# Two-layer trunk on one core: five of sixteen low weight parts in gate and up made by ScalarE's negated copy and an accumulating DMA inside SBUF

## The reference

```
x = x + concatenate([tok, cross]) @ w_out
x = x + swiglu(rms_norm(x, norm_ffn_g[i]), ffn_w_gate[i], ffn_w_up[i], ffn_w_down[i])
swiglu(h, w_gate, w_up, w_down) = (silu(h @ w_gate) * (h @ w_up)) @ w_down
```

## Time and profile before

| | |
|---|---|
| median of 3 runs | 2358.95 us |
| lowest and highest | 2358.91, 2359.38 us |
| profiled execution, span of its instructions | 2357.9 us |
| VectorE busy | 1734.6 us (74%) |
| ScalarE busy | 1239.5 us (53%) |
| GpSimd busy | 159.7 us (7%) |
| DMA | 441.14 MB, mean 187 GB/s |

### The profile page before, as it was taken

How to read it: one execution, slowest core, us unless ns; L and a number is a source line. 1 busy time by engine, 2 the same in 40 slices (tenths; PEclk the granted TensorE clock), 3 DMA queues, 4 the chain that set the end, 5 groups by cost and what they waited for, 6 DMA issues and landing times.

```text
span 2357.9 us, 29177 instructions
## 1 busy us (share of the span) xinstructions
PE 2350.1 (100%) x10566; PEld 1902.8 (81%) x10566; DVE 1734.6 (74%) x2131; ACT 1239.5 (53%) x1545; POOL 159.7 (7%) x114
## 2 busy tenths in 40 slices
PE   9999999999999999999999999999999999999999
PEld 7888888888788888888888888888888888888887
DVE  6555666656988888759898546655988888759887
ACT  7645555545655555545554554444655555545453
POOL 1000110000010010000000000000111020000000
PEclk9999999999999999999999999999999999999999
DMA  8654555445655556555556755555555655555564
GB/s 262 207 186 152 161 161 163 161 165 172 201 192 194 195 182 204 188 188 191 192 189 196 238 157 169 175 177 181 191 193 187 198 194 196 185 190 190 197 208 156
DMA packets 230691, 441.14 MB, mean 187 GB/s; under 512 B 14637, under 2 KB 18866, under 8 KB 230322
## 3 DMA queue, kind: packets, MB, share of 16 engines
q1 hardware_dynamic: 224274, 430.01, 55.8%
q10 hardware_dynamic: 6304, 9.61, 1.2%
HBM read 437.45 MB, written 2.12 MB: 186 GB/s over the span
## 4 chain that ended last, share of the span: by engine, by line
PE 98%; ACT 1%; DVE 1%; issue 0%; DMA 0%; POOL 0%; ACTq 0%; DVEq 0%
PE bank L598 26%; PE bank L597 25%; PE bank L596 25%; PE bank L691 6%; PE bank L693 6%; PE bank L692 5%; PE bank L618 2%; PE bank L813 1%; PE bank L838 0%; ACT w_hi L988 0%; PE bank L667 0%; PE bank L787 0%; PE bank L762 0%; PE bank L825 0%; ACT y L1057 0%
## 5 line engine op out<-in xcount | busy, mean ns | idle before, releaser
L1412 DVE TENSOR_TENSOR w_lo<-raw,w_hi 128x1024 fp32r<-128x1024 f32 (+1 forms) x816 | 961.7, 1191 | 556.5 <-ACT w_hi L988 555.0
L988 ACT ACTIVATE w_hi<-raw 128x1024 fp32r<-128x1024 f32 (+1 forms) x816 | 822.0, 1016 | 835.0 <-PE bank L598 798.3
L598 PE MATMUL bank<-w_hi,hT_lo 128*128 128x512 f32 x1680 | 669.5, 398 | 0.0
L596 PE MATMUL bank<-w_hi,hT_hi 128*128 128x512 f32 x1680 | 668.5, 398 | 0.0
L597 PE MATMUL bank<-w_lo,hT_hi 128*128 128x512 f32 x1680 | 661.8, 394 | 0.0
L597 PEld LDWEIGHTS bank<-w_lo,hT_hi 128*128 128x128 f32 x1680 | 315.6, 188 | 77.3
L596 PE MATMUL bank<-w_hi,aT_hi 128*128 128x512 f32 x944 | 374.4, 397 | 1.8 <-DVE w_lo L1412 1.8
L598 PE MATMUL bank<-w_hi,aT_lo 128*128 128x512 f32 x944 | 375.3, 398 | 0.0
L598 PEld LDWEIGHTS bank<-w_hi,hT_lo 128*128 128x128 f32 x1680 | 315.3, 188 | 73.6
L596 PEld LDWEIGHTS bank<-w_hi,hT_hi 128*128 128x128 f32 x1680 | 315.5, 188 | 73.0
L597 PE MATMUL bank<-w_lo,aT_hi 128*128 128x512 f32 x944 | 372.6, 395 | 0.0
(11 more groups left out here) (194 smaller groups left out, 2171.7 us busy)
## 6 DMA issues: line engine op xcount, KB each, us to landing
raw<-in_ffn_w_gate_dram SPq DMA_DIRECT2D x176, 512.0 KB, 3.5
raw<-in_ffn_w_up_dram SPq DMA_DIRECT2D x176, 512.0 KB, 4.3
raw<-in_ffn_w_down_dram SPq DMA_DIRECT2D x176, 512.0 KB, 4.4
raw<-in_a_w_in_dram SPq DMA_DIRECT2D x104, 512.0 KB, 3.5
raw<-in_b_w_in_dram SPq DMA_DIRECT2D x72, 512.0 KB, 3.7
raw<-in_a_w_out_dram SPq DMA_DIRECT2D x40, 512.0 KB, 3.5
raw<-in_b_w_out_dram SPq DMA_DIRECT2D x40, 512.0 KB, 4.1
raw<-in_mem_w_kv_dram SPq DMA_DIRECT2D x32, 512.0 KB, 4.4
```

The source lines that it names most:

```text
L596: nc.tensor.matmul(o, hi[:, k, rows], w_hi[:, slot, a, :], start=(first and a == 0), stop=False)
L598: last = nc.tensor.matmul(o, lo[:, k, rows], w_hi[:, slot, a, :], start=False, stop=(last_one and a == CHUNK_KT - 1))
L988: nc.scalar.activation(w_hi[:, slot, 0:tiles], raw[:, slot, 0:tiles], ACT.Copy).then_inc(hi_ready, 1)
L1412: nc.vector.tensor_tensor(w_lo[:, slot, 0:tiles], raw[:, slot, 0:tiles], w_hi[:, slot, 0:tiles].bitcast(F32), ALU.subtract).then_inc(chunk ...
```

## The change

In pairs 1 to 10 of each layer, for chunks 3, 6, 7, 10 and 11 (`ADDED`), `w_lo` is no longer made by VectorE. ScalarE writes `w_lo = Copy(-raw)`, rounded to fp32r as the high part is, ahead of its `w_hi = Copy(raw)`; then GpSimd issues a DMA that adds `raw` into `w_lo`, so that `w_lo` holds raw minus the high part. SyncE's next load of that slot waits for the DMA instead of for VectorE, and so does TensorE. VectorE skips these chunks. GpSimd does this for every pair behind its `sum_weights`, in the order 3, 6, 7, 10, 11; its loop over pairs is written out. SyncE's loop over pairs starts at pair 1, with pair 0 ahead of it.

```
+ADDED = (3, 6, 7, 10, 11)
...
+            kinds = collections.deque([False] * RING, RING)
+            def load(w, k0, first_col, added=False):
...
-                    sp.wait_ge(chunk_split, tally.at("chunk", 1 - RING))
+                    if kinds[0]:
+                        sp.wait_ge(hi_ready, tally.at("chunk", 1 - RING))
+                        sp.wait_ge(low_added[slot], tally.at(f"added{slot}") * 16)
+                    else:
+                        sp.wait_ge(chunk_split, tally.at("split", -sum(not kind for kind in list(kinds)[1:])))
...
+            def weights_ready(slot, added=False):
+                if added:
+                    pe.wait_ge(hi_ready, tally.at("chunk", 1))
+                    pe.wait_ge(low_added[slot], tally.at(f"added{slot}", 1) * 16)
+                    tally.add(f"added{slot}")
+                else:
+                    pe.wait_ge(chunk_split, tally.at("split", 1))
+                    tally.add("split")
...
                     if tally.turn is not None or ring_turn > 0:
                         act.wait_ge(chunk_used, tally.at("chunk", 1 - RING))
+                    if added:
+                        nc.scalar.activation(w_lo[:, slot], raw[:, slot], ACT.Copy, scale=-1.0).then_inc(negated, 1)
                     nc.scalar.activation(w_hi[:, slot, 0:tiles], raw[:, slot, 0:tiles], ACT.Copy).then_inc(hi_ready, 1)
...
-                    if not end or ahead < len(plan.seq):
+                    if 0 < pair < PAIRS and ahead in ADDED:
+                        tally.add("chunk")
+                    elif not end or ahead < len(plan.seq):
                         splits(1, 1 if ahead in plan.second else CHUNK_KT)
...
-                tally.n["chunk"] = start + plan_of(pair).first[0]
-                sum_weights(buffers(pair)[0], tally.at("seven", 0 if buffers(pair)[0] is buffers(pair - 1)[-1] else -1))
+                if plan_of(pair).sevens:
+                    tally.n["chunk"] = start + plan_of(pair).first[0]
+                if plan_of(pair).sevens:
+                    sum_weights(buffers(pair)[0], tally.at("seven", 0 if buffers(pair)[0] is buffers(pair - 1)[-1] else -1))
+                for c in ADDED:
+                    slot = c % RING
+                    tally.add("negated")
+                    pool.wait_ge(negated, tally.at("negated"))
+                    nc.gpsimd.dma_start(w_lo[:, slot].bitcast(F32), raw[:, slot], accum_op=ALU.add
+                                        ).then_inc(low_added[slot], 16)
...
-                    with pool.Fori(0, (LATE - 2) // TURN_PAIRS) as turn:
-                        tally.enter(turn)
-                        for pair in (1, 2):
-                            sum_pair(pair)
-                        tally.leave((LATE - 2) // TURN_PAIRS)
-                    for pair in range(LATE - 1, PAIRS - 1):
+                    for pair in range(1, PAIRS):
                         sum_pair(pair)
```

More of the change, by code:

```diff
@@ L13 @@
+import collections
 import math
@@ L416, in trunk @@
         mixes_made = sem("mixes_made")
+        negated = sem("negated")
+        low_added = [sem(f"low_added{s}") for s in range(RING)]
         mixes_hi = sem("mixes_hi")
@@ L426, in per_turn @@
         def per_turn(pairs):
-            return dict(chunk=PAIR_CHUNKS * pairs, t=pairs, y=pairs, split_t=2 * pairs, evac=pairs, sq=0, sums=0, pow=0,
+            by_slot = {f"added{s}": pairs * sum(c % RING == s for c in ADDED) for s in range(RING)}
+            return dict(by_slot, split=(PAIR_CHUNKS - len(ADDED)) * pairs, negated=len(ADDED) * pairs,
+                        chunk=PAIR_CHUNKS * pairs, t=pairs, y=pairs, split_t=2 * pairs, evac=pairs, sq=0, sums=0, pow=0,
                         step=(2 * len(GATE_UP.sevens) + 1) * pairs, seven=len(GATE_UP.sevens) * pairs, partial=pairs,
@@ L510, in _ @@
             tally = Tally(per_turn(1))
-            def load(w, k0, first_col):
+            kinds = collections.deque([False] * RING, RING)
+            def load(w, k0, first_col, added=False):
                 ring_turn, slot = ring_place(tally)
                 if tally.turn is not None or ring_turn > 0:
-                    sp.wait_ge(chunk_split, tally.at("chunk", 1 - RING))
+                    if kinds[0]:
[3 more added lines that the diff above has]
+                        sp.wait_ge(chunk_split, tally.at("split", -sum(not kind for kind in list(kinds)[1:])))
                 sp.dma_start(raw[:, slot], w[:, k0:k0 + CHUNK_KT, bass.ds(first_col, BLOCK)]
@@ L519, in load @@
                 tally.add("chunk")
+                tally.add(f"added{slot}" if added else "split")
+                kinds.append(added)
             def ktiles(w):
@@ L558, in _ @@
                     load_block(w_out[0], b, OUT_ORDER)
-                with sp.Fori(0, PAIRS) as pair:
+                for c in range(IN_CHUNKS):
+                    for w in (ffn_w_gate, ffn_w_up):
+                        load(ktiles(w[layer]), c * CHUNK_KT, 0)
+                with sp.Fori(0, PAIRS - 1) as pair:
                     tally.enter(pair)
                     for c in range(IN_CHUNKS):
-                        for w in (ffn_w_gate, ffn_w_up):
-                            load(ktiles(w[layer]), c * CHUNK_KT, pair * BLOCK)
-                    tally.leave(PAIRS)
+                        for g, w in enumerate((ffn_w_gate, ffn_w_up)):
+                            load(ktiles(w[layer]), c * CHUNK_KT, pair * BLOCK + BLOCK, 2 * c + g in ADDED)
+                    tally.leave(PAIRS - 1)
                 for half, plan in enumerate(DOWN):
@@ L576, in _, with product @@
             asked = dict(cross_scores=0, diff_scores=0, transposed=0)
-            def product(side_T, outs, c, order, first, last_one, ready=(), piece_ready=(), token_first=False):
+            def weights_ready(slot, added=False):
[6 more added lines that the diff above has]
+                    tally.add("split")
+            def product(side_T, outs, c, order, first, last_one, ready=(), piece_ready=(), token_first=False, added=False):
                 hi, lo = side_T
                 _, slot = ring_place(tally)
-                pe.wait_ge(chunk_split, tally.at("chunk", 1))
+                weights_ready(slot, added)
                 if c in ready:
@@ L698, in seven_first @@
                 _, slot = ring_place(tally)
-                pe.wait_ge(chunk_split, tally.at("chunk", 1))
+                weights_ready(slot)
                 k = u * CHUNK_KT
@@ L752, in run_pair @@
                         product(side_T, (adds[g], adds[2 + g]), u, range(plan.units), u == 0, u == plan.units - 1,
-                                token_first=(end and c == len(plan.seq) - 1))
+                                token_first=(end and c == len(plan.seq) - 1), added=(0 < pair < PAIRS and c in ADDED))
                 t_banks[0] = T_BANKS
@@ L979, in _, with splits @@
             tally = Tally(per_turn(TURN_PAIRS))
-            def splits(count, tiles=CHUNK_KT):
+            def splits(count, tiles=CHUNK_KT, added=False):
                 for _ in range(count):
@@ L1163, in run_pair @@
                     elif not end or ahead < len(plan.seq):
-                        splits(1)
+                        splits(1, added=(0 < pair < PAIRS and ahead in ADDED))
                     if c not in early:
@@ L1981, in _ @@
         def _(pool):
-            tally = Tally(dict(step=2 * TURN_PAIRS, chunk=PAIR_CHUNKS * TURN_PAIRS, seven=len(GATE_UP.sevens) * TURN_PAIRS))
+            tally = Tally(dict(step=2 * TURN_PAIRS, chunk=PAIR_CHUNKS * TURN_PAIRS, seven=len(GATE_UP.sevens) * TURN_PAIRS,
+                               negated=len(ADDED) * TURN_PAIRS))
             def link(ins):
```

## The result

The changed kernel takes 2485.16 us in the median of 4 runs (2478.73 to 2487.48) against 2359.09 for the kernel before on the same chip. The ratio is 1.053, 95% interval 1.0517 to 1.0543. That is 126 us slower where 98 were forecast.

A forecast was written before the change was run, and what follows sets the result against it. TensorE was taken as the bound, hurt only by late low parts. Stalls of 5.6 us in pairs 1 to 7 and 4.9 in 8 and 9 gave 98.0 us over two layers: 2457 us, own range 2390 to 2545.

The forecast's parts named there:

- VectorE's time is worth nothing: Five splits a pair leave VectorE, 123 us in all; all of it lies beside matmuls, so worth 0.
- chunk 3 waits because its add stands behind the sum of weights: On GpSimd the add of chunk 3 is issued after the sum: 2.7 us of stall in pairs 1 to 9.
- A: Time an add takes from issue to landing: taken as 6 us, ends kept 3.2 and 8.8.
- the rival of the slow transfer: Adds take 7 us or more, by GpSimd's issuing or a full DMA: 235 us slower, 2594; chance 0.18.
- The lead of 3.3 us: Slack of chunk 3: from its add's issue at 793.05 to TensorE's start of the chunk at 796.37.
- what adding costs the transfer: An add fetches w_lo as well as raw, twice the bytes in: 1.7 us more than a load's 4.3.
- Slot 2 (6, then 10) has no such stall: Chunks 6 and 10: the add of 6 lands before the shifted start of chunk 6, so no stall.
- the stalls of 7 and 11: In slot 3, chunks 7 and 11 stall by 1.4 and 1.5 us a pair; 0.8 for 11 in pairs 8 and 9.
- the burst of loads (7, 8 and 9): SyncE holds these loads until chunk 3's add lands, then issues them together; their sums and splits had about 3 us spare.
- the chain of slot 3: Between its chunks 3, 7 and 11 the slot needs a load, a negated copy and an add: L + 1.06 + A against 10.59 us.
- The top of the range: Slow end of the forecast's own range: 3.7 + 3.2 + 3.3 = 10.2 us a pair, about 190 us, 2545.
- L: Time a chunk's load takes to land: taken as 4.8 us, ends kept 3.5 and 6.

The follow-up runs named there:

- Experiment 5: The changed kernel with adds for chunks 10 and 11 alone: 2360.50 us, ratio 1.0006.
- 1: The changed kernel with GpSimd issuing the add of chunk 3 ahead of its sum of weights: 2420.48 us, ratio 1.0271.
- 4: The changed kernel with one add a pair, for chunk 3 alone: 2372.32 us, ratio 1.0059.
- experiment 3: The changed kernel with the DMA copying raw into w_lo in place of adding it: 2364.28 us, ratio 1.0026.
- Experiment 7: The changed kernel with adds for chunks 3, 7 and 11 alone, all in slot 3: 2423.10 us, ratio 1.0279.
- 9: The changed kernel with adds for chunks 3 and 6 alone, sum of weights first: 2433.98 us, ratio 1.0322.
- 12: The changed kernel with adds for chunks 3 and 6 alone, that of 3 ahead of the sum of weights: 2370.74 us, ratio 1.0049.
- 8: The changed kernel with adds for chunks 3, 6, 11 and 14, that of 3 ahead of the sum; SyncE's loop begins at pair 2: 2429.52 us.
- 10: The changed kernel with adds for chunks 3, 6 and 14, that of 3 ahead of the sum; SyncE's loop begins at pair 2: 2376.99 us.
- 11: The changed kernel with adds for chunks 7 and 10 alone, in different slots: 2418.67 us, ratio 1.0252.
- experiment 6: The changed kernel with adds for chunks 6 and 10 alone, both in slot 2: 2368.51 us, ratio 1.0036.
- 2: The changed kernel with adds for 6, 7, 10 and 11, chunk 3 on VectorE again: 2408.99 us, ratio 1.0204.

## Why the prediction was right or wrong

**Right: VectorE's time is worth nothing.** Experiment 5 takes 40 splits from VectorE and gives the time of before. The bound was TensorE, and no version here is faster than the kernel before.

**Right: chunk 3 waits because its add stands behind the sum of weights.** Experiments 1 and 4 show it. The term was too large: 2.7 us a pair forecast, 1.6 measured in the changed kernel (29.5 over 18), 0.7 with chunk 3 alone. A was 4.6 there, not 6, as the DMA engines were quiet, which the rival of the slow transfer had noted and the sum had not used. The lead of 3.3 us was nearly right, by two changes that the sum did not have: it is 3.9 with chunk 3 alone, because the sum of weights got shorter, and 3.0 in the changed kernel, where that sum waits for a load that comes later and so starts 0.8 us later in the pair.

**Nearly right: what adding costs the transfer.** The shortest landing is 2.9 us for the copies of experiment 3 and 4.5 for the adds of the changed kernel: 1.6 us apart, of which 0.3 is GpSimd's longer issue and 1.3 the transfer, where the prediction took 1.7 for the second operand. The Trainium skill, page "Collectives: The Full Stack", section "The bandwidth ceiling: the fold count and why AG ≠ RS ≠ AR", says that a reducing transfer reads two sources for each write and so runs at about half a copy's rate. Experiment 3 agrees with the half: 2.7 us of the DMA engines for an add, 1.3 for a copy.

**Wrong: "Slot 2 (6, then 10) has no such stall", and the stalls of 7 and 11.** Where 1.4 and 1.5 us a pair were put to chunks 7 and 11, they had about 3.5 us in all 20 pairs; chunks 6 and 10, at which nothing was forecast, took 69 us. Two things failed in that step. It took one A for all adds, while it ran from 4.5 to 9.5; the text had the burst of loads (7, 8 and 9) in it, but let it delay the sums, not the add that is issued into it. And it let the stalls add up: a stall ahead of 6 gives chunk 7 the same time, so the chain of slot 3 was covered. Experiment 7, where chunk 6 covers nothing, shows 1.1 us a pair ahead of 11 but only 0.3 ahead of 7, whose adds land there in 5.3 us in the median and not in 6. That chunk 6's stall is the burst's is shown by 9 and 12, and that the same happens in two other places by 8 and 10 and by 5 and 11. The prediction had named stalls at 6 and 10 as a sign that it was wrong, and in this step it was.

**Missing: the clock.** No term was made for it, as no row of before shows a stall in a pair. 15 stretches at 1.2 GHz cost about 22 us.

**Small things.** The top of the range was added up wrongly: with A of 7 and L of 5.5 the stalls of 7 and 11 are 3.1 and 3.2 us, 10.0 a pair and about 180 in all, not 10.2 and 190. VectorE is down by 108 us and not 123, ScalarE up by 95 and not 106; neither bears on the time.

That the total came out near the truth, 98 against 126, is luck: a chain that was covered by earlier stalls, and an A too large for chunk 3, stood in for a burst and a clock that were not counted.

**Open:** how exactly the 40 us ahead of chunk 10 divide. Both the chain (6 to 10 in one slot, experiment 6: 9 us alone) and the burst (7 holds 11, 12 and 13, experiment 11: 60 us) can do it. The traces say that both are in it and that the landing weighs more. Over pairs 1 to 9 the add of 10 is issued 5.3 us ahead of the need and lands in 7.3; in experiment 5, without either, these are 6.3 and 5.2, in experiment 6, with the chain alone, 5.5 and 5.7. So the later issue takes 0.9 us a pair and the longer landing 2.2, less the 1.1 that experiment 5 had to spare: about the 2.1 us of stall measured. How much of the landing is due to the add of 11, issued some 2 us behind it, is not shown; in experiment 5 two such adds land in 5.9 us at most. A version in which the held loads go by another queue, so that an add holds only its own slot, was not tried.

## What to carry to other kernels

Where one engine issues all loads in order, a wait put in front of one load delays all behind it and then releases them together. Ask what is issued at that moment: here it was the next critical transfer, and it took nearly twice its time. Before moving work to the DMA engines look at the share in short windows, not the mean: 0.80 over the pairs still meant 0.98 in the burst shown. And work taken from an engine that TensorE did not wait for gained nothing here.

## What the runs showed of the hardware

- An add of 512 KB inside SBUF issued by GpSimd lands 4.5 to 4.8 us after issue when little else moves, and up to 9.6 when loads fill the engines. A copy lands in 2.9 at best, 3.9 in the median. The issue itself takes 0.87 us of GpSimd for an add and 0.54 for a copy. In every version with adds it stays between 0.86 and 1.06 us, so what stretches a landing comes behind it.
- Sharing: an add issued 0.6 us after the first of three loads took 8.7 us; the load of chunk 7 itself, issued first, landed in 4.2. The Trainium skill, page "DMA: Bandwidth & Descriptors", section "Queues, rings and completion order", says that each DMA engine takes turns between the queues for which it has work, packet by packet. An add that is stretched while loads go on agrees with it; no run here shows the packets' order.
- The granted clock was 1.00 in all windows of 1 us of the first layer's pairs in the kernel before, in experiment 1 (stalls up to 2.3 us) and in experiment 3. In the changed kernel it fell to 0.50 eight times in that layer, each time at the end of a stall of 1.8 to 2.9 us or within 1.5 us of it, and for 3 to 4 us; but not with each stall of that length (2.59 us of idle time ahead of 694.42 and, in the second layer, 3.40 ahead of 1975.49 were followed by none).
- GpSimd's sum of two operands of 512 columns took 1.30 us where it was 2.17 with VectorE's split of chunk 3 beside it, and that split took 2.03 in place of 1.23. In experiments 2, 5 and 11, where VectorE makes that split again, the sum is back at 2.16 us in the median.
